# All 22 chunks of each down projection by seven products, with two slots of the weight loads exchanged

## The reference

```
def swiglu(x, w_gate, w_up, w_down):
    return (jax.nn.silu(x @ w_gate) * (x @ w_up)) @ w_down
...
x = layer_norm(ALPHA * x + 0.5 * swiglu(x, ffn1_w_gate[l], ffn1_w_up[l], ffn1_w_down[l]), ln_g[l, 0], ln_b[l, 0])
proj = x @ w_in[l]                 # then pooling, gated convolution, neighbourhood attention
y = jnp.concatenate([y_a, y_b, y_c], axis=-1) @ w_out[l]
x = layer_norm(ALPHA * x + y, ln_g[l, 1], ln_b[l, 1])
x = layer_norm(ALPHA * x + 0.5 * swiglu(x, ffn2_w_gate[l], ffn2_w_up[l], ffn2_w_down[l]), ln_g[l, 2], ln_b[l, 2])
```

## Time and profile before

| | us |
|---|---|
| median of 3 runs | 2957.13 |
| lowest and highest | 2955.15, 2959.99 |
| the profiled execution | 2963.7 |
| its span in the trace | 2961.8 |
| PE busy in it | 2855.8 (96%) |
| DVE busy | 1594.2 (54%) |
| ACT busy | 1094.6 (37%) |

### The profile page before, as it was taken

The page is one execution under the profiler, slowest core; times in us unless marked ns, Lnnn a source line. Parts: engine busy times, 40 slices in busy tenths (PEclk is TensorE's granted clock), DMA queues, the critical chain, the costliest instruction groups (busy, mean ns, idle before and its releaser), DMA issues.

```text
span 2961.8 us, 34169 instructions
## 1 busy us (share of the span) xinstructions
PE 2855.8 (96%) x14401; PEld 2375.5 (80%) x14401; DVE 1594.2 (54%) x2211; ACT 1094.6 (37%) x1416; POOL 118.8 (4%) x123
## 2 busy tenths in 40 slices
PE   7999998999999989999999999999999999999998
PEld 7888877887887878878876878888888886788886
DVE  4345357734535665453556574635745364656455
ACT  4322443432234333232545432324323354543332
POOL 0020000001000000000100000000000010000000
PEclk9999999999999999999999999999999999999999
DMA  5242122323221223443521343423534351234342
GB/s 217 72 128 84 59 77 80 98 71 114 72 86 57 72 90 115 145 117 111 102 100 38 107 127 128 131 97 114 143 114 131 111 102 58 73 113 142 110 132 86
DMA packets 67816, 305.19 MB, mean 103 GB/s; under 512 B 6916, under 2 KB 7106, under 8 KB 40016
## 3 DMA queue, kind: packets, MB, share of 16 engines
q1 hardware_dynamic: 53216, 263.21, 26.1%
q0 software_dynamic: 12992, 32.00, 5.7%
q10 hardware_dynamic: 1456, 7.80, 0.9%
HBM read 294.60 MB, written 2.10 MB: 100 GB/s over the span
## 4 chain that ended last, share of the span: by engine, by line
PE 80%; DVE 10%; ACT 4%; DMA 4%; issue 2%; ACTq 0%; SPq 0%; DVEq 0%; POOLq 0%
PE G L483 14%; PE G L485 14%; PE G L484 14%; PE G L495 7%; PE G L497 7%; PE G L496 7%; DMA raw<-in_stream 3%; DVE w_lo L1675 2%; PE G L957 2%; PE G L959 2%; PE G L958 2%; ACT w_hi L1118 1%; PE A L1008 1%; PE A L1030 1%; PE A L670 1%
## 5 line engine op out<-in xcount | busy, mean ns | idle before, releaser
L483 PE MATMUL G<-xT_hi,w_hi 128*128 128x512 f32 (+1 forms) x2368 | 880.8, 372 | 17.7 <-DVE x L2232 6.0
L485 PE MATMUL G<-xT_hi,w_lo 128*128 128x512 f32 (+1 forms) x2368 | 869.7, 367 | 0.0
L484 PE MATMUL G<-xT_lo,w_hi 128*128 128x512 f32 (+1 forms) x2368 | 869.2, 367 | 0.0
L1675 DVE TENSOR_TENSOR w_lo<-raw,w_hi 128x2048 fp32r<-128x2048 f32 (+1 forms) x218 | 497.9, 2284 | 495.5 <-ACT w_hi L1118 495.2
L1118 ACT ACTIVATE w_hi<-raw 128x2048 fp32r<-128x2048 f32 (+1 forms) x218 | 413.2, 1896 | 696.4 <-PE G L485 366.2
L483 PEld LDWEIGHTS G<-xT_hi,w_hi 128*128 128x128 f32 x2368 | 448.8, 190 | 90.3 <-DVE x L2232 6.6
L485 PEld LDWEIGHTS G<-xT_hi,w_lo 128*128 128x128 f32 x2368 | 448.5, 189 | 73.3
L484 PEld LDWEIGHTS G<-xT_lo,w_hi 128*128 128x128 f32 x2368 | 449.1, 190 | 68.8
L495 PE MATMUL G<-w_hi,xT_hi 128*128 128x512 f32 (+1 forms) x512 | 193.3, 378 | 7.5 <-DVE xT_lo L2252 2.7
L497 PE MATMUL G<-w_hi,xT_lo 128*128 128x512 f32 (+1 forms) x512 | 186.1, 364 | 0.0
L496 PE MATMUL G<-w_lo,xT_hi 128*128 128x512 f32 (+1 forms) x512 | 185.9, 363 | 0.0
(11 more groups left out here) (315 smaller groups left out, 3651.7 us busy)
## 6 DMA issues: line engine op xcount, KB each, us to landing
raw<-in_stream SPq DMA_DIRECT2D x208, 1024.0 KB, 4.9
raw<-in_stream SPq DMA_DIRECT2D x80, 512.0 KB, 5.5
raw<-in_stream POOLq DMA_DIRECT2D x32, 512.0 KB, 9.7
lnr<-in_ln_rows POOLq DMA_DIRECT2D x6, 1024.0 KB, 5.2
row<-in_rows POOLq DMA_DIRECT2D x6, 512.0 KB, 7.1
x<-in_x ACTq DMA_DIRECT2D x1, 2048.0 KB, 17.9
tB<-fA ACTq DMA_DIRECT2D x4, 512.0 KB, 5.4
xn<-fB ACTq DMA_DIRECT2D x4, 512.0 KB, 8.4
```

Source lines behind the costliest of these rows:

```text
L483: mm(o, a, hi[:, c, at:at + n], start=start and own_start, stop=False, **k)
L484: mm(o, a, lo[:, c, at:at + n], start=False, stop=False, **k)
L485: return mm(o, wl[:, col:col + P], hi[:, c, at:at + n], start=False, stop=stop, **k)
L1675: tt(w_lo[:, s, 0:nk, :], raw[:, r, 0:nk, :], w_hi[:, s, 0:nk, :].bitcast(F32), ALU.subtract).then_inc(lo_done, 1)
```

## The change

All three parts are now done by seven products, in the order 4, 3, 4 units (`FF_PARTS`, `SUMMED`), and `h_hi`, `h_lo`, `w3_hi`, `w3_lo` and `LAST_DOWN` are gone. A product of the three-unit part has 18 matmuls, and its blocks and sums are three quarters as large.

```
-SUMMED = 2
-LAST_DOWN = (4, 2)
-FF_HALVES = ((4, (4, 4)), (4, (4, 4)), (3, LAST_DOWN))
+FF_HALVES = ((4, (4, 4)), (3, (4, 2)), (4, (4, 4)))
+SUMMED = len(FF_PARTS)
```

Two loads exchange slots. `raw[0]`'s second content is now the quarter for product 4, and `raw[1]`'s the quarter onto which POOL adds t3 for product 5; the loads of the next blocks into `raw[0]` and `raw[1]` follow products 4 and 5 (SP, then POOL):

```
-                    alternate(raw[:, 0], b + 2, 0, (half_in[0], raw_in[0]))
+                    alternate(raw[:, 0], b, 1, (half_in[0], raw_in[0]), units)
+                    taken(first + 4)
+                    slot_free()
+                    alternate(raw[:, 1], b + 2, 0, (half_in[1], raw_in[1]), units)
                     taken(first + 5)
-                    slot_free()
-                    alternate(raw[:, 1], b, 1, (half_in[1], raw_in[1]))
-                    taken(first + 4)
...
-                pool.wait_ge(half_in[0], 32 * p + 32)
-                pool.wait_ge(raw_in[0], (ring // 2 + 2) * 16)
-                add_from(raw[:, 0], b + 2, 1, t3_sum)
+                pool.wait_ge(half_in[1], 32 * p + 32)
+                pool.wait_ge(raw_in[1], (ring // 2 + 2) * 16)
+                add_from(raw[:, 1], b + 2, 1, t3_sum, units)
                 pool.wait_ge(lo_done, split + 5)
-                add_from(raw2[:, 0], b, 1, t4_sum)
+                add_from(raw2[:, 0], b, 1, t4_sum, units)
```

In the last part of each feed forward the norm is woven into the products (`last_products`, `half_stats`, `measured_summed` on DVE, `layer_norm_summed` on ACT). The first two tiles' sums are complete after product 4; their statistics are made there, their scale comes behind a read of product 5 and ahead of the next block's split, and PE transposes them between the two tiles of product 6:

```
+            def last_products(L, n, units):
+                inner, eps = L < 3 * DEPTH - 1, 4.0 * LN_EPS
...
+                split_summed(raw2[:, 0], units)
+                Pos.fewer += 3
+                read_product(5, n, (0,))
+                if inner:
+                    scaled(0)
+                    scaled(1)
+                    read_product(5, n, (1,))
+                    for i in range(2):
+                        half_stats(5, i)
+                    split()
+                    low_parts(L, 0, (0, 1))
+                    read_product(6, n, (0,))
+                    measured_summed(6, 0, eps)
+                    split()
+                    low_parts(L, 0, (2, 3))
+                    scaled(2)
+                    read_product(6, n, (1,))
+                    measured_summed(6, 1, eps)
+                    scaled(3)
+                    low_parts(L, 1, range(4))
+                else:
+                    read_product(5, n, (1,))
+                    param(dve, L // 3, "ln_in", L % 3 + 1, 3)
+                    result(0, (slice(0, 1024),))
+                    result(1, (slice(0, 1024),))
+                    for i in range(2):
+                        half_stats(5, i)
+                    for i in range(2):
+                        read_product(6, n, (i,))
+                        measured_summed(6, i, eps)
+                        result(2 + i, (slice(0, 512), slice(512, 1024)) if i else (slice(0, 1024),))
```

On ACT:

```
+            def layer_norm_summed(L):
+                if L == 3 * DEPTH - 1:
+                    for t in range(TILES):
+                        rsqrt(1, t, preload=False)
+                    return
+                for t in range(2):
+                    rsqrt(1, t, preload=False)
+                for t in range(2):
+                    scale_normed(L, t)
+                split()
+                normed_operand(L, 0, (0, 1))
+                split()
+                normed_operand(L, 0, (2, 3))
+                normed(L, 2)
+                normed(L, 3)
+                normed_operand(L, 1)
```

The evacuation of the fourth tile stood last before too, but of bank 3 (it waits for the last matmul of all); the read that stands there now is of bank 1. Where the next block's first job but one uses bank 1, it now waits for this read:

```
+                                if bank in Pos.held:
+                                    pe.wait_ge(S["st_read"], Pos.held.pop(bank))
```

More of the change, by code:

```diff
@@ L366, in pieces, with alternate @@
                 Q.split += 1
[L368 to L372, removed]
+            def alternate(place, b, odd, signals, units):
+                for o, n in enumerate((2, units - 2)):
+                    sp.dma_start(place[:, 2 * o:2 * o + n, :],
+                                 stream[b + o:b + o + 1].rearrange("o p (k e n) -> (o p) k e n", e=2, n=BC)[:, 0:n, odd, :]
                                  ).then_inc(signals[o], 16)
@@ L635, in gemm_last_half @@
                 for i, (b, t, k0, k1) in enumerate(order):
[L636 to L637 removed]
+                    s = (Pos.off + b) % 2
+                    wh, wl = w_hi[:, s], w_lo[:, s]
                     if first[b] == i:
@@ L918, in ffn, with products @@
                             gain_columns()
[L919 to L932, removed]
+                    products(units, L if n == SUMMED - 1 else None)
+                    N.ff += 3 * units
+            def products(units, L=None):
+                inner = L is not None and L < 3 * DEPTH - 1
+                for k in range(PRODUCTS):
+                    s, a = Pos.off % 2, BANKS[k]
+                    pe.wait_ge(lo_done, 2 * Pos.pair + Pos.off + 3)
+                    for i in range(2):
+                        if inner and k == PRODUCTS - 1 and i == 1:
                             pe.wait_ge(S["ln_c"], 1)
@@ new lines, in ffn @@
+                        act.wait_ge(g_free[2], Pos.ubase + Pos.u + 2)
+                        fn(hs[:, u, 0, 0, :], work[:, 1024:1280], ACT.Copy).then_inc(S["ff_hi"], 1)
+                        if before_products:
+                            act.wait_ge(S["w_sum"], 2 * N.parts + 1)
+                            split(units)
+                        N.sums += 1
+                        act.wait_ge(S["ff_sum"], N.sums)
+                        fn(hs[:, u, 0, 3:7, :], work[:, 0:1024].rearrange("p (a t) -> p a t", a=4),
+                           ACT.Copy).then_inc(S["ff_hi"], 1)
@@ L1506, in ffn @@
+                        act.wait_ge(g_free[3], Pos.ubase + Pos.u + 2)
+                        fn(hs[:, u, 0, 1:3, :], work[:, 1536:2048].rearrange("p (a t) -> p a t", a=2),
+                           ACT.Copy).then_inc(S["ff_hi"], 1)
+                        N.ff += 3
                         if not before_products:
-                            split(LAST_DOWN[1] if n == SUMMED and u == units - 1 else KB)
+                            split()
                         Pos.u, Pos.end = Pos.u + 1, Pos.end + 2
@@ new lines, in ffn @@
+                    act.wait_ge(raw_in[0], ((2 * Pos.pair + Pos.off - 2 - Pos.fewer) // 2 + 1) * 16)
+                    split_summed(raw[:, 0], units)
+                    if last and bias_rows:
+                        bias_rows(1)
+                    act.wait_ge(t3_sum, 32 * (N.parts + 1))
+                    split_summed(raw[:, 1], units)
+                    act.wait_ge(t4_sum, 32 * (N.parts + 1))
+                    split_summed(raw2[:, 0], units)
+                    Pos.fewer += 3
+                    N.parts += 1
@@ L2639, in _ @@
                 load_ln(2)
-                sums_of_weights(l, 1, 0)
-                sums_of_weights(l, 1, 1)
+                for part in range(SUMMED):
+                    sums_of_weights(l, 1, part)
 def weight_stream(v):
```

297 lines of the change are left out of this document (107 added, 190 removed).

## The result

| | us | ratio to before |
|---|---|---|
| changed kernel, median of 4 runs | 2976.67 (2970.95 to 2978.47) | 1.0057, interval 1.0045 to 1.0068 |
| before, beside it, 4 runs | 2956.56 (2955.15 to 2959.99) | |
| changed kernel again, 5 runs | 2974.58 (2970.64 to 2978.24) | 1.0051, interval 1.0038 to 1.0064 |
| forecast | 2946 (2934 to 2960) | 0.996 |

What follows compares the result with a forecast made beforehand. The prediction took PE, busy 2855.8 of 2961.8 us, and its few waits to bound the kernel. Its terms summed to -11.2 us, from a median of 2957.1 to 2946, range 2934 to 2960.

Steps and rivals of the forecast that it cites:

- 72 matmuls fewer: Four down projections on PE: 18 matmuls fewer in each, at 0.2267 us apiece, -16.3 us.
- waits for product 4, and the clock behind one: Product 4's weight, loaded earlier into the other slot: PE's waits and one spell at the lower clock go, -9.5 us.
- products 5 and 6, three units: Parts of three units: product 6 waits 0.5 us for its weight in each of four, +2.0 us.
- product 6, four units: Parts of four units: product 6's weight lands at 26, needed at 28.4 after product 0; no wait.
- starts of products: Product 1 waits for an ordinary split beside DVE's sums, in twelve parts instead of eight: +1.0 us.
- hand-over L=0, 3: Hand-over from the feed forward to what follows, after L=0 and 3: +0.6 us each, +1.2 in all.
- hand-over L=2, waits: Hand-over after L=2: PE's second job waits 4.7 us for bank 1; waits in all +4.0 us.
- lower clock behind its second wait: After L=2, behind the wait for bank 1: the granted clock falls, costing 1.7 us.
- tail: Kernel's end: 16.0 us behind PE's end in place of 11.2, +4.7 us.
- Products 5 and 6: Step on the last two products' weight loads: no wait in four units, 0.5 us per part of three, +2.0 us.
- Rival (c): Product 6: ring load and its weight load share engines at once, weight 4.1 us later everywhere; +28, 2974 us; chance 0.11.
- Rival (b): Parts of three units: product 6 waits 2.5 us, two lose 1.6 of clock; +11, 2957 us; chance 0.17.

Runs made afterwards that it cites:

- after_again: The changed kernel once more, unaltered: 2974.58 us in 5 runs, ratio to before 1.0051.
- before_again: The kernel before, unaltered, profiled a second time: one run of 2956.6 us, span 2954.7.
- ring_after_t4: The changed kernel with the next block's first ring load held until product 6's weight (t4) has landed: ratio to before 1.0002.
- swap_ring: The kernel before with the two slot loads exchanged and the next ring load held until product 6's weight has landed: ratio to before 0.9993.
- after: The changed kernel itself, first group: median 2976.67 us in 4 runs, ratio to before 1.0057.
- no_swap: The changed kernel with the exchange of the two slot loads undone: ratio to before 1.0014.
- read_early: The changed kernel with DVE's read of product 6's second tile moved ahead of the second split at the hand-over: ratio to before 1.0028.

## Why the prediction was wrong, term by term

Measured is what the traces after_again and before_again show at the place, start to start.

| step | forecast | measured |
|---|---|---|
| 72 matmuls fewer | -16.3 | -16.3 |
| waits for product 4, and the clock behind one | -9.5 | -1.6, and +1.0 that stays |
| products 5 and 6, three units | +2.0 | +2.8 and +11.0, +3.3 of clock |
| product 6, four units | 0 | +4.8 |
| starts of products | +1.0 | -0.7 |
| hand-over L=0, 3 | +1.2 | +0.4 |
| hand-over L=2, waits | +4.0 | +3.5 |
| lower clock behind its second wait | +1.7 | +2.5 |
| tail | +4.7 | +4.5 |
| lower clock elsewhere (one stretch more) | 0 | +1.6 |
| ahead of the first of these parts | 0 | +1.3 |
| sum | -11.2 | +18.1, as in the spans |

The rows are good to a few tenths each. The last two have nothing to do with the change as far as these traces show.

**The step that failed** is "Products 5 and 6": "a load of SP's behind a running accumulation stands still from 1307 to 1310 at least, and by then t4 is nearly in". The row was right and the conclusion was not. A load that stands still for some 3.5 us from its issue and then moves with three quarters of the engines is one load; issued at P0 + 16 it moves at P0 + 20, while t4 needs the engines until 22 at best. The landing of t4 itself was put too early as well: 21.2 in the forecast, 21.6 to 23.7 in the four parts of ring_after_t4, where no ring load runs beside it, and 24.0 to 25.5 in the eight of the two traces of the changed kernel. So t4 was 1.4 us later than worked out, on average, even with nothing of SP's beside it, which is more than the slack of 0.1 to 0.5 at product 6, and the ring load added 2. Why it was late by itself I did not trace. I had the second half before me (84% from 1314 on) and used it only for the rival. In the parts of four units I wrote "t4 five later at 26. No wait" and left the ring load out, though it is issued at P0 + 21: t4 landed at 28.2 to 29.8 in seven of the ten such parts of the two traces that a plain hand-over to the next part follows, and the slack of 2.4 was gone. Rival (c) named the place, the points from which it decides (21.3 and 28.4) and 2974; it was given 0.11, and it had the load begin at once, which it doesn't. Rival (b) had the parts of three units right almost to the number, 2.5 for product 6 in each and the lower clock in two of four; its total of 2957 missed because the gain of product 4 wasn't there and the parts of four units waited too. That the total came out near (c)'s is in part luck.

The Trainium skill, "DMA: Bandwidth & Descriptors", section "Queues, rings and completion order", has the engines take turns between queues, a packet at a time. The trace of the kernel before agrees where both queues have work for long: from 1312 to 1314, both with packets of 2 KB, they send 128 and 118.

```profile
q0 software_dynamic: 128, 0.26, 71.6%
q1 hardware_dynamic: 118, 0.24, 36.6%
```

It doesn't agree for the first 3.5 us of the ring load, in which SP's queue had a load issued and at most 2 packets moved. So the forecast had read the stretch from 1307 to 1310 rightly; what it had wrong was how long such a stretch lasts.

**The second error** is a size. The waits for product 4 were read from one execution, 7.0 in five waits; the next one had 0.8. A usual value lies between, and swap_ring puts the whole term at 2 to 3 us in place of 9.5. Nothing in the first trace says that it is a bad draw but its time: 2963.7 with a median of 2957.1, a difference that I wrote down and then did not use.

**Right** were the hand-overs and the tail, in mechanism and nearly in size. PE's first and second job after L=2, and DVE's read of bank 1:

```profile
2016.47 0.36 PE L472 MATMUL G<-xT_hi,w_hi 128*128 128x256 f32 x1 [1.58 <-DVE x L2317]
...
2022.48 0.55 PE L472 MATMUL G<-xT_hi,w_hi 128*128 128x256 f32 x1 [4.34 <-DVE x L2317]
```

```profile
2021.57 0.16 DVE L2202 SCALAR_TENSOR_TENSOR nmx<-mean_var,rs_r 128x1 f32<-128x1 f32 x1
2021.65 0.68 DVE L2317 TENSOR_TENSOR x<-x,G 128x512 f32<-128x512 f32 x1
```

4.6 from start to start against 4.7 forecast, with product 6 begun at 2006.9 and the read done at Q + 15.4 against 15.8. The lower clock behind it came as forecast, and cost 2.5 rather than 1.7: PE's matmuls of half width start 0.21 apart until 2028, 0.12 in the job before. At the end, the last matmul and DVE's last pass:

```profile
2953.20 0.39 PE L931 MATMUL G<-w_hi,hs 128*128 128x512 f32 x1
```

```profile
2965.28 1.41 DVE L2227 SCALAR_TENSOR_TENSOR x<-x,rs_r,lnr 128x512 f32<-128x512 f32 x2
```

2969.1 - 2953.4 = 15.7 behind PE, against 16.0 forecast and 11.2 before.

So of the 4.1 us that 18 matmuls save in each down projection, 3.5 go to waits in its part of three units and 2 more to product 6 of the other parts and to the clock behind the waits; the hand-over at L=2, the lower clock behind it and the tail take 10.5 on top, once for the whole kernel.

## What to carry to other kernels

A load that is issued earlier is not free because nobody waits for it: ask which transfer on the critical path is still under way when it begins to move, and hold it until that one has landed. Here one wait on a semaphore was worth 15 us, nearly as much as 72 matmuls. Where two queues take turns packet by packet, the one with the larger packets should get the larger part of the bytes (an estimate from the rows: 8 KB of SP's took an engine 0.32 us, 2 KB of POOL's 0.15); no run here varied the packets. And a term that rests on waits of one execution needs a second one, above all where the profiled execution is slower than the median.

## What the runs showed that I had not expected

- A ring load that is issued beside a running accumulation first stands still for some 3.5 us and then takes three quarters of the engines. The last 256 KB of t4 took 3.6 to 4.8 us beside it, 1.4 to 3.4 with it held (ring_after_t4) and 1.2 to 1.7 where t4 comes early (no_swap).
- A wait alone does not tell whether the lower clock follows. Behind waits of 2.3 to 2.9 us for product 6 it came in two of four parts in each trace of the changed kernel. Behind the wait of 4.3 for bank 1 at L=2 it came in all four traces that have that wait (after, after_again, ring_after_t4, no_swap). The stretches behind a wait of 2.6, behind a like one and behind 4.34 (column PEclk):

```profile
1309.70:1312.70 3.00, 2.97 (x13) 2.52 (x14) 3.00 (x3) 0.00 (x0) 0.00 (x0) 1.00 0.00 0
2246.00:2249.00 3.00, 3.00 (x10) 2.35 (x9) 2.29 (x3) 0.00 (x0) 0.00 (x0) 0.58 0.00 0
2022.40:2025.00 2.60, 2.52 (x12) 2.55 (x13) 1.82 (x8) 1.05 (x4) 0.00 (x0) 0.50 0.52 221
```

Behind the first the clock stayed full, and the second ran ten matmuls in 3.0 us, where the first ran 13. In read_early, without the wait of 4.34:

```profile
2017.00:2021.00 4.00, 3.79 (x30) 3.65 (x31) 3.93 (x6) 3.90 (x9) 0.00 (x0) 1.00 0.51 215
2021.00:2026.00 5.00, 5.00 (x44) 5.00 (x43) 3.59 (x15) 1.99 (x5) 0.00 (x0) 1.00 0.60 210
```
